# RWKV time mixing on one core: decay and rate products on 128 rows, and the chain's keys and deltas stacked over 128 rows

## The chip, the cores and the metric

The kernel runs on one core of one Trainium2 chip. The metric is the device time in microseconds of one execution; several executions are made and the median is taken. The profile is of one execution, taken by the hardware profiler.
## The reference, cut to what matters

The model has two layers over 256 context and 512 latent tokens of width 1024: layer 0 is grouped-query attention, layer 1 bidirectional RWKV-7 time mixing, each followed by an MLP. The change lies in the RWKV part of layer 1:

```python
w_log = -softplus(-(w0 + tanh(xw @ w1) @ w2)) - 0.5     # two directions n, rank 64
a = sigmoid(a0 + (xa @ a1) @ a2)                        # two directions, rank 64
k_dir = k * (1 + (a - 1) * k_a)
decay = exp(-exp(w_log))
def step(S, inp):                                       # per direction and head (16 heads of 64)
    w_t, k_t, v_t, a_t, b_t = inp[:5]                   # a_t = -kk, b_t = kk * a
    sa = einsum('dbhij,dbhj->dbhi', S, a_t)
    S = S * w_t + sa[:, None] * b_t + v_t[:, None] * k_t
    return S, einsum('dbhij,dbhj->dbhi', S, inp[5])     # times r
```

The decay product is `tanh(xw @ w1) @ w2` with `w0` added, the rate product is `(xa @ a1) @ a2`. The state takes two outer products, one of the keys with the values and one of `b` with the deltas `sa`.

## The kernel before

The RWKV core works through 16 units q: 8 groups g of 128 channels (two heads) times two directions d. The scan is done in 12 chunks of 64 tokens (`C = 64`), two chunks `cp` to a tile `m` of 128 tokens. Each unit goes through three stages, and `slots` runs them shifted against each other: slot s holds `pre(s)`, `inverse(s - 1)` and `chain(s - 2)`. The order inside a slot is written out by hand in two strings `SLOT` of the letters p, i and c; at each letter every engine emits its next piece of that stage. So every engine's queue has this fixed order, and each waits by semaphores for the others. Slots 0 to 15 have a pre stage, the chain runs alone at the end.

`pre` (lines 882 to 1096): PE makes the decay product into PSUM. `w0` goes in as a product of a row of ones with `W0G` on one row of the array (L890), and `W2G` times the tanh tile `LW` on 64 rows adds to it (L894): the two directions lie in the upper and lower 64 partitions of `LW`, `LA`, `W2G` and `A2G`, and each q takes its half. ACT takes the tanh (L984), PE makes the rate product on the same 64 rows (L901), ACT its tanh (L988), PE the cumulative product over the tokens of a chunk (L908, 128 rows), ACT two exponentials. HEAD1 sums squares (L917), VG is transposed (L925) and copied by ACT into `VT` (L1008). DVE makes BT = kk * a * WI and KD = k_dir * WI; PE transposes both into `BKT` (L934, L942) and multiplies them with `AR` into the 64x64 matrices of `MT` (L958), which DVE masks (L1093). L971 multiplies `MT` with V into `LV`.

`inverse` (L1119 to L1163): 19 rounds of 64x64 products (L1124, L1129, L1144) with copies by DVE (`UM`) and ACT. Neighbours stand in different quarters of the array.

`chain` (L1208 to L1255) walks through the 12 chunks. Each step has three pieces. First, `AR` times the state `SS` (L1224), and DVE adds `LV` to give `RH`. Second, the inverse times `RH` gives the deltas (L1236), DVE copies them to `SA` (L1318), and in the shadow of that copy PE multiplies keys and V into the state's PSUM (L1241). Third, PE waits for `SA`, adds its product with `BKT` (L1248), and for the last 8 chunks adds two products to the output, one with V (L1253) and one with `SA` (L1256). DVE makes the new `SS`. V and SA of one chunk stand on the same 64 partitions, so all of these products have 64 rows and 64 columns.

SP loads per group KG, W2G, A2G and W0G (counted by `ga_loaded`, L1461) and then VG, RG and G2G (L1466). The first load waits for the end of the low-rank products (`w_used`). POOL sets pads of `WP` to 1 at the start (L1507, L1508).

## Time and profile before

| | us |
|---|---|
| median of 3 runs | 2772.3 (2768.23 to 2775.69) |
| profiled execution | 2781.47, its span 2779.5 |
| TensorE busy | 2500.7 (90% of the span) |
| DVE, ACT, POOL busy | 1107.7, 952.6, 573.2 |
| mean granted clock of TensorE | 0.922 |

The RWKV core takes the stretch from about 1373 to 2340 us of the span. Times in the views are from the span's start. Ends of products are modelled, so neighbouring records overlap. In the timeline a row stands for one or more records of one line; in the chain of waits a row gives the piece of a group that lies on the chain.

### The profile page before, as it was taken

Reading aid. Unit: us, or ns where it says so; the run is one execution under the profiler, and the core shown is the slowest. Engines: PE = TensorE matmul, PEld = TensorE weight load, DVE = VectorE, ACT = ScalarE, POOL = GpSimd, SP = SyncE. Lnnn points to the kernel's source line nnn. Section 1 sums busy time; section 2 is a strip of 40 time slices with the busy share of each in tenths; the row PEclk is TensorE's granted clock in tenths of the full one; section 3 lists DMA queues with packets and bytes.
Section 4 is the critical chain, followed back from the end, with each engine's and each line's share of the span. In section 5 each row is a group of like instructions: output and inputs, shape, how many; then the busy total and the mean of one; then the engine's idle time right before and its main releaser. Section 6 shows DMA issues by size and latency. Waiting matters only on the chain.

```text
span 2779.5 us, 67680 instructions
## 1 busy us (share of the span) xinstructions
PE 2500.7 (90%) x28879; PEld 2062.0 (74%) x28879; DVE 1107.7 (40%) x2324; ACT 952.6 (34%) x1605; POOL 573.2 (21%) x361
## 2 busy tenths in 40 slices
PE   5989998899999998699678999998999986899998
PEld 4767777788888887587457777777777774788886
DVE  2235655231212122522735565555655553311112
ACT  3655555231212122222333334333332332323323
POOL 0320000222232322222111111111111101344442
PEclk9999999999999999799869899988988895999999
DMA  7225453211111211124100000000000001232331
GB/s 224 57 66 168 152 171 89 61 61 61 60 60 60 71 55 56 53 93 120 59 20 3 21 11 13 20 4 21 11 13 20 3 3 54 69 106 91 96 99 60
DMA packets 172290, 176.11 MB, mean 63 GB/s; under 512 B 26240, under 2 KB 159760, under 8 KB 172048
## 3 DMA queue, kind: packets, MB, share of 16 engines
q1 hardware_dynamic: 172048, 172.49, 19.8%
q8 instruction: 200, 3.28, 0.5%
q14 instruction: 42, 0.34, 0.0%
HBM read 160.93 MB, written 11.53 MB: 62 GB/s over the span
## 4 chain that ended last, share of the span: by engine, by line
PE 83%; DVE 9%; issue 4%; ACT 2%; DMA 1%; SPq 0%; POOL 0%; ACTq 0%; DVEq 0%; PEldq 0%
PE PS L379 43%; PE PS L1144 5%; PE PS L399 3%; PE PS L607 2%; PE PS L1129 2%; PE PS L958 2%; PE PS L634 2%; PE PS L901 2%; PE PS L908 2%; PE PS L1124 1%; PE PS L1248 1%; PE PS L1236 1%; PE PS L1224 1%; PE PS L586 1%; PE PS L894 1%
## 5 line engine op out<-in xcount | busy, mean ns | idle before, releaser
L359 POOL TENSOR_TENSOR WL<-RAW,WH 128x1024 fp32r<-128x1024 f32 x184 | 439.7, 2413 | 1340.6 <-ACT WH L353 1340.6
L379 PE MATMUL PS<-AH,WH 128*128 128x512 f32 (+1 forms) x1320 | 475.1, 360 | 84.0 <-DVE AL L824 38.4
L379 PE MATMUL PS<-AH,WL 128*128 128x512 f32 (+1 forms) x1320 | 473.8, 359 | 0.0
L379 PE MATMUL PS<-AL,WH 128*128 128x512 f32 (+1 forms) x1320 | 469.8, 356 | 0.0
L379 PEld LDWEIGHTS PS<-AH,WH 128*128 128x128 f32 x1320 | 253.9, 192 | 133.1 <-issue 55.2
L379 PEld LDWEIGHTS PS<-AL,WH 128*128 128x128 f32 x1320 | 252.7, 191 | 37.3
L379 PEld LDWEIGHTS PS<-AH,WL 128*128 128x128 f32 x1320 | 253.6, 192 | 33.9
L353 ACT ACTIVATE WH<-RAW 128x1024 fp32r<-128x1024 f32 x184 | 183.8, 1047 | 267.1 <-PE PS L379 265.5
L379 PE MATMUL PS<-BH,WL 128*128 128x512 f32 (+1 forms) x768 | 273.4, 356 | 0.0
L379 PE MATMUL PS<-BH,WH 128*128 128x512 f32 (+1 forms) x768 | 272.6, 355 | 0.0
L379 PE MATMUL PS<-BL,WH 128*128 128x512 f32 (+1 forms) x768 | 271.5, 353 | 0.0
L549 DVE SCALAR_TENSOR_TENSOR X<-PS,MOD,X 128x256 f32 (+3 forms) x120 | 72.0, 656 | 447.2 <-PE PS L379 447.2
L1144 PE MATMUL PS<-XI,MT 64*64 64x64 f32 x3840 | 189.9, 233 | 7.4 <-issue 6.1
L1129 PE MATMUL PS<-XIT,UM 64*64 64x64 f32 x3840 | 180.5, 226 | 16.0 <-issue 15.8
L525 DVE TENSOR_TENSOR HSQ<-HRL 128x768 f32<-128x768 f32 (+1 forms) x64 | 51.2, 841 | 332.6 <-ACT HRL L513 332.6
L1144 PEld LDWEIGHTS PS<-XI,MT 64*64 64x64 f32 x3840 | 160.1, 144 | 17.8 <-issue 17.3
L1129 PEld LDWEIGHTS PS<-XIT,UM 64*64 64x64 f32 x3840 | 146.1, 136 | 23.9 <-issue 23.7
L379 PEld LDWEIGHTS PS<-BH,WH 128*128 128x128 f32 x768 | 144.9, 189 | 21.9
L379 PEld LDWEIGHTS PS<-BL,WH 128*128 128x128 f32 x768 | 144.4, 188 | 21.4
L1174 ACT ACTIVATE XI<-PS 128x256 f32<-128x256 f32 x192 | 73.5, 383 | 251.6 <-PE PS L1129 251.5
L379 PEld LDWEIGHTS PS<-BH,WL 128*128 128x128 f32 x768 | 144.7, 188 | 20.2
L1111 POOL TENSOR_TENSOR MT<-MT,CT 128x256 f32<-128x256 f32 x48 | 34.9, 727 | 575.3 <-DVE MT L1093 575.3
(239 smaller groups left out, 4601.5 us busy)
## 6 DMA issues: line engine op xcount, KB each, us to landing
ADW<-l_ada_w SPq DMA_DIRECT2D x40, 1024.0 KB, 5.3
RAW<-l_mlp_up SPq DMA_DIRECT2D x64, 512.0 KB, 4.3
RAW<-l_mlp_down SPq DMA_DIRECT2D x64, 512.0 KB, 4.0
RAW<-l_w_rkv SPq DMA_DIRECT2D x24, 512.0 KB, 4.7
rwkv_scratch<-STG SPq DMA_DIRECT2D x24, 384.0 KB, 2.7
ADA<-l_ada_w SPq DMA_DIRECT2D x4, 2048.0 KB, 15.8
RAW<-l_w_in SPq DMA_DIRECT2D x16, 256.0 KB, 5.4
RAW<-l_w_out SPq DMA_DIRECT2D x16, 256.0 KB, 5.1
```

Source lines behind the costliest of these rows:

```text
L353: e.activation(WH[:, s, rows], RAW[:, s, rows], ACT.Copy).then_inc(w_high[h], 1)
L359: e.tensor_tensor(WL[:, s, rows], RAW[:, s, rows], WH[:, s, rows], ALU.subtract).then_inc(w_split[h], 1)
L379: mm = e.matmul(dst, w[:, s, k, n * P:(n + 1) * P], r[:, k, lo:hi], start=(k == 0 and i == 0), stop=(k == KT - 1 and i == 2), skip_group_c ...
L399: mm = e.matmul(dst, w[:, s, k, n * P:(n + 1) * P], r[:, k, lo:hi], start=(k == 0 and i == 0), stop=(k == KT - 1 and i == 2), skip_group_c ...
L549: ins = e.scalar_tensor_tensor(out=x, in0=tile_ps(4 * s + 2 * n)[:, a0:a1], scalar=gate, in1=x, op0=ALU.mult, op1=ALU.add)
L607: mm = e.matmul(pair(2 * j)[:, a0:a1], QS[:, g % 2, j, r * P:(r + 1) * P], kk[:, j, a0:a1], start=(i == 0), stop=(i == 1), skip_group_chec ...
L634: mm = e.matmul(bank(7)[64 * j:64 * j + 64, 0:P], VF[:, 2 * p + j, l, :], PTS[:, m % 2, b, :], start=(l == 0), stop=(l == nb - 1), skip_gr ...
L901: mm = e.matmul(tile_ps(3)[:, a0:a1], A2G[r, :], LA[r, a0:a1], start=True, stop=True, skip_group_check=True)
L908: mm = e.matmul(pair(3)[:, m * P:(m + 1) * P], SG[:, m, :], table(f"cum{d}"), start=True, stop=True, skip_group_check=True)
L1129: return e.matmul(bank(2)[o if v < 15 else HALVES[cp], i * C:(i + 1) * C], UM[o, v % 2, i, :], XIT[o, 4 * (v % 3) + i, :], start=True, sto ...
L1144: mm = e.matmul(bank(0)[o, i * C:(i + 1) * C], MT[b][t, u, 0, 0, :], XI[t, u, :] if n >= 3 else IDN[t, t], start=True, stop=True, skip_gro ...
L1174: e.activation(XI[:, four, :].rearrange("p u t -> p (u t)"), bank(1)[:, 0:256], ACT.Copy).then_inc(xi_ready, 1)
```

## The change

The two directions get tiles of their own, filled up with zeros: `LW[d]` is [128, T], with the tanh on its own 64 partitions, a row of ones on the first partition of the other half and zeros elsewhere; `W2X[:, d]` has `w2` on the same 64 rows and `w0` on the row of the ones. `A2X[:, d]` has `a2` on 64 rows and zeros on the others. The product of the ones is gone, and decay and rate products use all 128 rows. POOL makes the zeros and ones, and SP and ACT wait for it (`PADS = 12`); SP's loads per group go from 4 to 7 for `ga_loaded`. The LW tanh becomes two on 64 partitions each.

In the chain, `VSA` has a slot for each chunk with V on one half of the partitions and the deltas on the other. BT and KD are laid out as `KB` so that in `BKT` each chunk has keys on V's half and BT on the deltas' half, and `MT` has its output matrices stacked in the same way. State and output products of a chunk become one each with 128 rows in place of two with 64. To put the deltas there, `RH`, `LV`, the inverse's operands and the results move to the other half. The V copy becomes two ACT instructions of 64 partitions, `UM` moves into unused places of `AR`, masks grow by 128 columns for each direction, and `AA = KK * AA` is made in place.

```diff
 def pe_pre(e, q):
-    e.wait_ge(ga_loaded, 64 * (g + 1) + 16)
+    e.wait_ge(ga_loaded, 112 * (g + 1) + 16)
-    for m0, m1 in ((0, 4), (4, NTT)):
-        e.matmul(pair(3)[:, m0 * P:m1 * P].rearrange("p (m c) -> p m c", c=P), ONES[0:1, :],
-                 W0G[0:1, d, :].unsqueeze(1).to_broadcast([1, m1 - m0, P]), start=True, stop=False,
-                 skip_group_check=True)
-        for m in range(m0, m1):
-            mm = e.matmul(pair(3)[:, m * P:(m + 1) * P], LW[r, m * P:(m + 1) * P], W2G[r, :], start=False,
-                          stop=True, skip_group_check=True)
+    for m in range(NTT):
+        mm = e.matmul(pair(3)[:, m * P:(m + 1) * P], LW[d][:, m * P:(m + 1) * P], W2X[:, d, :], start=True,
+                      stop=True, skip_group_check=True)
...
-        mm = e.matmul(tile_ps(3)[:, a0:a1], A2G[r, :], LA[r, a0:a1], start=True, stop=True, skip_group_check=True)
+        mm = e.matmul(tile_ps(3)[:, a0:a1], A2X[:, d, :], LA[:, a0:a1], start=True, stop=True, skip_group_check=True)
...
-                for i, src in enumerate((BT, KD)):
-                    for cp, t in enumerate(HALVES):
+                for i in range(2):
+                    for cp in range(2):
                         c = 2 * m + cp
                         for h, k in enumerate(HEADS):
-                            mm = e.matmul(bank(3 + h)[t, i * P:i * P + wide * C], src[k, c * C:(c + 1) * C],
-                                          AR[b][k, c, 0:wide, :].rearrange("p a t -> p (a t)"), start=True, stop=True,
-                                          skip_group_check=True)
+                            out = bank(3 + h)[HALVES[1 - cp] if i == 0 else HALVES[cp], :].rearrange("p (z t) -> p z t", t=C)
+                            mm = e.matmul(out[:, i:i + 1, :] if wide == 1 else out[:, i:3 + cp:2 + cp - i, :],
+                                          KB[k, m, 1 + cp if i == 0 else 3 * cp, :], AR[b][k, c, 0:wide, :], start=True,
+                                          stop=True, skip_group_check=True)
 def act_pre(e, q):
-                e.activation(VT[gp][:, :, :].rearrange("p m c -> p (m c)"), pair(3)[:, 0:T], ACT.Copy).then_inc(vt_ready, 1)
+                for cp, t in enumerate(HALVES):
+                    ins = e.activation(VSA[gp][t, cp::2, :], pair(3)[t, 0:T].rearrange("p (m c) -> p m c", c=P), ACT.Copy)
+                ins.then_inc(vt_ready, 1)
 def pe_chain(e, q):
-                if j < NCH - 1:
-                    for k in HEADS:
-                        e.matmul(bank(6)[k, P:P + HD], BKT[b][t, m, 1, k], VT[gp][t, m, k], start=True, stop=False,
-                                 skip_group_check=True)
                 yield
                 e.wait_ge(sa_ready, 12 * q + j + 1)
                 e.nop(nofuse=True)
                 if j < NCH - 1:
                     for k in HEADS:
-                        mm = e.matmul(bank(6)[k, P:P + HD], BKT[b][t, m, 0, k], SA[t, k], start=False, stop=True,
+                        mm = e.matmul(bank(6)[k, P:P + HD], BKT[b][:, m, cp, k], VSA[gp][:, c, k], start=True, stop=True,
                                       skip_group_check=True)
                     mm.then_inc(st_done, 1)
                 if j >= NCH - NX:
                     for h, k in enumerate(HEADS):
-                        e.matmul(bank(7)[k, out_cols], VT[gp][t, m, k], MT[b][t, 2 * m + h, 1, 1, :], start=False,
-                                 stop=False, skip_group_check=True)
-                    for h, k in enumerate(HEADS):
-                        mm = e.matmul(bank(7)[k, out_cols], SA[t, k], MT[b][t, 2 * m + h, 0, 1, :], start=False,
+                        mm = e.matmul(bank(7)[k, out_cols], VSA[gp][:, c, k], mt(b, 2 * m + h, 2 + cp), start=False,
                                       stop=(d == 1), skip_group_check=True)
 def _(sp):
+            sp.wait_ge(pads_ready, PADS)
...
-                                     (W2G[:, :], a["l1_w2"].rearrange("d r c -> (d r) c")[:, cols]),
-                                     (A2G[:, :], a["l1_a2"].rearrange("d r c -> (d r) c")[:, cols]),
-                                     (W0G[:, :, :], a["l1_w0"][:, cols].unsqueeze(0))):
+                                     (W2X[0:64, 0, :], a["l1_w2"][0, :, cols]),
+                                     (W2X[64:128, 1, :], a["l1_w2"][1, :, cols]),
+                                     (W2X[64:65, 0, :], a["l1_w0"][0:1, cols]),
+                                     (W2X[0:1, 1, :], a["l1_w0"][1:2, cols]),
+                                     (A2X[0:64, 0, :], a["l1_a2"][0, :, cols]),
+                                     (A2X[64:128, 1, :], a["l1_a2"][1, :, cols])):
 def _(act):
-            act.activation(LW[:, :], tile_ps(0), ACT.Tanh).then_inc(evac_act, 1)
+            act.wait_ge(pads_ready, 4)
+            act.activation(LW[0][0:64, :], tile_ps(0)[0:64, :], ACT.Tanh)
+            act.activation(LW[1][64:128, :], tile_ps(0)[64:128, :], ACT.Tanh).then_inc(evac_act, 1)
```

## Rows read from the trace of the kernel before

**Rows 1.** The page: TensorE's clock in 40 slices, and the chain by engine.
```profile
PEclk9999999999999999799869899988988895999999
...
PE 83%; DVE 9%; issue 4%; ACT 2%; DMA 1%; SPq 0%; POOL 0%; ACTq 0%; DVEq 0%; PEldq 0%
```

**Rows 2.** The chain of waits, rate product L901 (start us, us, what, records).
```profile
1385.96 2.94 PE PS L901 x4
...
1475.65 2.85 PE PS L901 x4
...
2206.50 2.85 PE PS L901 x4
```

**Rows 3.** Windows: A:B length, busy PE PEld DVE ACT POOL, clock, DMA share, GB/s.
```profile
1476.00:2206.00 730.00, 667.18 (x15523) 553.10 (x15524) 422.82 (x1074) 259.56 (x520) 97.12 (x123) 0.88 0.05 13
1746.00:1750.50 4.50, 4.50 (x49) 3.10 (x47) 0.91 (x3) 0.60 (x2) 3.60 (x5) 1.00 0.01 4
1750.50:1753.50 3.00, 3.00 (x49) 2.74 (x49) 1.75 (x6) 0.81 (x1) 0.00 (x0) 0.52 0.00 0
...
1758.00:1760.90 2.90, 2.90 (x14) 2.63 (x13) 0.63 (x2) 0.00 (x0) 0.00 (x0) 0.51 0.02 6
1760.90:1765.00 4.10, 4.08 (x137) 3.73 (x136) 2.80 (x9) 2.75 (x6) 0.00 (x0) 1.00 0.00 0
1430.00:1440.00 10.00, 9.39 (x80) 7.06 (x79) 2.21 (x5) 2.17 (x3) 0.00 (x0) 0.50 0.01 2
2296.00:2332.00 36.00, 25.23 (x270) 19.93 (x268) 11.84 (x44) 0.00 (x0) 0.00 (x0) 0.51 0.01 1
```

**Rows 4.** Timeline of PE through one decay product (start us, us, line, form, records).
```profile
1746.99 1.12 PE L890 MATMUL PS<-W0G,ONES 1*128 1x512 f32 x2
1748.04 1.16 PE L894 MATMUL PS<-W2G,LW 64*128 64x128 f32 x8
...
1750.39 0.27 PE L1224 MATMUL PS<-SS,AR 64*64 64x64 f32 x2
```

**Rows 5.** Groups by line: the decay product's (busy us, mean ns).
```profile
L894 PE MATMUL PS<-W2G,LW 64*128 64x128 f32 x192 | 37.3, 339 | 0.0
...
L890 PE MATMUL PS<-W0G,ONES 1*128 1x512 f32 (+1 forms) x64 | 34.2, 619 | 6.3 <-DMA W0G<-l_w 5.7 <-ACT LV L1031 0.4
```

**Rows 6.** Timeline of PE around L917, a product on 128 rows.
```profile
1708.89 0.33 PE L1248 MATMUL PS<-SA,BKT 64*64 64x64 f32 x4
1709.15 1.56 PE L917 MATMUL PS<-TB,CK 128*128 128x256 f32 x4
1710.64 0.27 PE L1124 MATMUL PS<-UM,XIT 64*64 64x64 f32 x1
...
1710.80 0.22 PE L1124 MATMUL PS<-UM,XIT 64*64 64x64 f32 x1
...
1710.86 0.22 PE L1124 MATMUL PS<-UM,XIT 64*64 64x64 f32 x1
```

**Rows 7.** Timeline of PE in one third piece of the chain.
```profile
1766.28 0.33 PE L1248 MATMUL PS<-SA,BKT 64*64 64x64 f32 x4
1766.42 0.25 PE L1253 MATMUL PS<-MT,VT 64*64 64x64 f32 x2
...
1766.53 0.22 PE L1256 MATMUL PS<-MT,SA 64*64 64x64 f32 x1
```

**Rows 8.** Waits from 1476 to 2206 us (us in total, times, longest).
```profile
PE PS L1248 <- DVE SA L1318: 4.0, 11, 0.4
```

**Rows 9.** Groups by line: the V copy on ACT.
```profile
L1008 ACT ACTIVATE VT<-PS 128x768 f32<-128x768 f32 x8 | 6.5, 809 | 10.4 <-PE PS L925 10.4
```

**Rows 10.** Timeline of all engines at the core's start.
```profile
1373.07 0.34 SPq L1451 DMA_DIRECT2D CT<-table  x1
...
1375.50 0.73 SPq L1461 DMA_DIRECT2D W0G<-l_w  x1
...
1378.73 2.04 PE L890 MATMUL PS<-W0G,ONES 1*128 1x512 f32 x2 [5.75 <-DMA W0G<-l_w]
```

More of the change, by code:

```diff
@@ L222, in build @@
         VG, RG = two("VG", [P, T]), two("RG", [P, TX])
-        W2G, A2G, G2G = core("W2G", [P, P]), core("A2G", [P, P]), two("G2G", [P, P])
-        W0G = core("W0G", [1, 2, P])
+        W2X, A2X, G2G = core("W2X", [P, 2, P]), core("A2X", [P, 2, P]), two("G2G", [P, P])
         KK = core("KK", [P, T])
         WI = core("WI", [P, T])
-        bt_at = core_at[0]
-        SG = core("SG", [P, NTT, P])
-        BT = place("BT", bt_at, [P, T])
-        kd_at = core_at[0]
+        SG = place("SG", core_at[0], [P, NTT, P])
+        KB = core("KB", [P, NTT, 4, C])
         AA = core("AA", [P, T])
-        KD = place("KD", kd_at, [P, T])
         TB = core("TB", [P, T])
-        UM = core("UM", [P, 2, 4, C])
         XI = core("XI", [P, 12, C])
@@ L237, in build @@
         RKS = two("RKS", [P, TX])
-        VT = two("VT", [P, NTT, P])
+        VSA = two("VSA", [P, NCH, P])
         AR = three("AR", [P, NCH, 2, C])
@@ L242, in build @@
         BKT = three("BKT", [P, NTT, 2, P])
-        MT = three("MT", [P, 12, 2, 2, C])
+        MT = three("MT", [P, 40 * C])
+        UM = [AR[b][:, 0:4, 1, :] for b in (1, 2)]
         LV = three("LV", [P, NTT, P])
@@ L859, in chunks, with mt_at, mt, lta @@
             return ap.rearrange("p (c t) -> p c t", t=C)
-        def lta(b, u0, u1):
-            return MT[b][:, u0:u1, 0, 0, :]
+        def mt_at(u):
+            m, h = divmod(u, 2)
+            return 256 * m + 128 * h if m < TC // P else 512 * (m - 1) + 256 * h
+        def mt(b, u, part):
+            return MT[b][:, mt_at(u) + part * C:mt_at(u) + part * C + C]
+        def lta(b, u0):
+            end = mt_at(u0 + 4) if u0 < 8 else 40 * C
+            return MT[b][:, mt_at(u0):end].rearrange("p (u z) -> p u z", u=4)[:, :, 0:C]
         HEADS = (slice(0, 64), slice(64, 128))
@@ L1184, in dve_inverse @@
                     i = n % 3
[L1185 removed]
+                    dst = UM[n % 2] if n >= 3 else XI[:, 4 * i:4 * i + 4, :]
                     e.wait_ge(u_done, 18 * q + n + 1)
@@ L1504, in _ @@
                     pool_split(pool, 2 * i + s, s)
+            for d in range(2):
+                pool.memset(LW[d][:, :], 0.0).then_inc(pads_ready, 1)
+            pool.wait_ge(pads_ready, 2)
+            pool.wait_ge(w_split[1], U_OUT1 + 2)
+            pool.memset(LW[0][64:65, :], 1.0).then_inc(pads_ready, 1)
+            pool.memset(LW[1][0:1, :], 1.0).then_inc(pads_ready, 1)
             pool.wait_ge(w_used, U_LORA + 4)
+            pool.wait_ge(pads_ready, 4)
+            for w in (W2X, A2X):
+                pool.memset(w[:, :, :], 0.0).then_inc(pads_ready, 1)
             for b in range(3):
```

84 lines of the change are left out of this document (44 added, 40 removed).

## Prediction

> **What bounds the kernel now.** I began with the page. TensorE carries 83% of the chain that ended last, and its clock row is full except in the RWKV part [rows 1]. The change touches nothing else, so I went to that part. In the chain of waits, the rate product (L901) stands once in each slot, so it measures the slot: 13 slots lie between the starts of its first and last row shown, (2206.50 - 1475.65) / 13 = 56.2 us each [rows 2]. The windows view then says what a slot is made of [rows 3]. From 1476 to 2206 TensorE is busy 667 of 730 us, so it is the bound; its clock averages 0.88. The clock has two levels, 1.2 and 2.4 GHz, so the share at 1.2 GHz is 2 x 0.12, which is 175 us or 13.5 us a slot. While the clock is low TensorE is busy all the time (3.00 of 3.00, 2.90 of 2.90), so what falls into it is paid at double price. At the high clock it idles 63 of 555 us, 11%.
>
> Where is the clock low? In one slot [rows 3], it is 1.00 while the decay product runs, 0.52 right behind it, 0.51 through the cumulative product L908, and 1.00 after that; the rate product L901 lies in between. The stretch from 1430, which holds L901 and L908 of the second slot, has 0.50. L901's rows are as long at the end of the stretch as at its start, 2.85 [rows 2]. So the clock falls at or just after the decay product, and comes back at L908, the first product on all 128 rows. The decay product is K=1 and K=64 work: L890 uses one row of the array, L894 and L901 use 64 [rows 4]. The inverse and the chain use 64x64 tiles, several side by side, and hold 1.00 for long stretches (1760.9 to 1765). My reading, a theory so far: before the clock falls the engine works on few rows with no neighbour beside it, and before it rises it works on all rows.
>
> **The change, part by part, for one steady slot.**
>
> *Decay product.* It goes from 16 issued rows (L890 four, L894 twelve; each fp32 product is two records) to the twelve of L894, now on 128 rows. Before: in the timeline it runs from 1746.99 to the next product at 1750.39, 3.4 us [rows 4]. In all slots L890 and L894 are busy 34.2 + 37.3 = 71.5 us [rows 5]; less some 7.5 for the first slot, over 15 that is 4.3, and 4.1 without the overlap of the two. After: eight L894 rows take 1.16 us from first start to last end [rows 4], so a start each 0.11; four more give 1.6, or 1.5 to the next start. Rows used don't lengthen a row: L917 on 128 rows streams its 768 columns in 1.5 us [rows 6]. -2.6 us (ends -1.9 and -2.8).
>
> *Rate product.* Same columns, 128 rows in place of 64. Before 2.85 us, in the low stretch [rows 2, 3]. After, if the clock holds, it is L917's 1.5 [rows 6]. -1.35.
>
> *Cumulative product (L908), not touched.* 2.86 us low, [rows 3] has its window; 1.5 at the high clock by the same 0.11 a start. -1.35.
>
> *The rest of the low time.* 13.5 us less 2.85, 2.86 and about 1.2 of the decay product leaves 6.6; half is 3.3. At the high clock the waits on ACT and DVE come out from under it, 11% and about half a microsecond between rate and cumulative product, where the tanh on ACT is late next. -2.5 (ends -1.5 and -3.3).
>
> *Falls that remain.* Slots also begin with a wait for instructions, and the chain alone can thin the work; I add back 2.8 us of low time a slot. +1.4 (0 to +3).
>
> *V products of the chain (L1241, L1253) removed.* 11 + 8 = 19 pairs for each q. In one step L1248, L1253 and L1256 start 0.14 and 0.11 apart [rows 7], so a pair is worth 0.12: -2.3. As they use half the rows and the inverse can run beside them, the lower end is half of that; the upper is with low clock in it (-1.1 to -2.9).
>
> *Change of array shape, added.* This is what the diff does not say. Third pieces of the chain become 128x64 while all around them is 64x64. At a change of shape the trace shows the array emptied: L1248 ends at 1709.22 by its row and the 128-row L917 starts at 1709.15, and L917 ends at 1710.71 and the 64x64 rows start at 1710.64, 0.07 before it each time. Inside one shape, rows 0.22 long start 0.06 after the group before, an overlap of 0.16, and the first row behind a change is 0.27 long, not 0.22, while it waits for weights [rows 6]. So one change costs 0.09 + 0.05 = 0.14 us. Twelve steps with a way in and a way out are 24 changes, 3.4 us. Little of it is covered: TensorE waited for SA before L1248 only 11 times, 4.0 us in 13 slots [rows 8]; those waits and neighbours that change shape anyway take off a tenth. No row shows a 128x64 product in this part, so the bounds are half the price (covers I do not see) and 0.25 each, if the inverse's four tiles side by side fill slowly again: +3.1 (+1.2 to +6).
> The Trainium skill, TensorEngine Tiling (Array Packing), Key Properties, says that switching tiling mode drains TensorE while switching tile does not. The rows above agree with it and give it its price here; without the drain this part would be a gain of 2.3 us a slot instead of a loss of 0.8, some 47 us over the kernel. By that rule this half of the change works against itself.
>
> *Products that stay.* A pair on all rows can't have the inverse beside it: 19 x 0.03 = +0.5 (0 to +1.1).
>
> *Small things.* The V copy on ACT becomes two on half the partitions; time goes by columns, so +0.81 us every second slot [rows 9]. ACT is busy 260 of 730 us [rows 3], so half of it is covered: +0.2. The pairwise products of L958 meet the same tile twice in a row: +0.2. On DVE, sizes stay the same; the write of UM in runs of 64 and KB likewise: 0, covered by DVE's 42% idle. (ends 0 and +0.8 together)
>
> Sum: -2.6 - 1.35 - 1.35 - 2.5 + 1.4 - 2.3 + 3.1 + 0.5 + 0.4 = -4.7 us a slot; over the 15 slots with a decay product after the first, -71.
>
> *First slot and start.* The clock is low throughout and the work waits step by step, so only the decay product counts: it starts at 1378.73 [rows 10] and the rate product follows at 1385.96 [rows 2], 7.2 us later; twelve rows at the low clock need about 3, as L908 does: -4.2. Against that, KG and the rest now wait for POOL's zeroing and there are seven loads in place of four. The last of four was issued at 1375.50, 2.4 us behind CT, the three more at 0.5 us each: +1.8, as TensorE waited for just that load. The wait stands on SP, and VG, RG and G2G queue behind it, which are wanted only behind the cumulative product. The LW tanh in two halves adds 0.8 on ACT, hidden by the same wait of 5.75 us. Net -2.4. The added loads of later groups are issued half a slot ahead: 0.
>
> *Tail.* From 2296 the chain runs alone at 0.51 [rows 3]. There the array is empty between steps anyway, so neither the changes nor the V products count (they run under the copy of SA): 0 to +2, taken as +0.5.
>
> Sum: -73 us. The profiled execution took 2781.5 us (span 2779.5 and 2.0 around it), 9.2 over the median 2772.3. 2781.5 - 73 = 2708.5, and against the median **2699**.
>
> **Rivals.**
> 1. *The clock keeps falling.* The low clock may come from the waits at the slot's head, not from the rows in use. For: from 1430 the clock is 0.50 with TensorE busy 9.4 of 10 us, so busy alone doesn't lift it. Against: it is 1.00 during the decay product and falls behind it, with no idle time between (4.50 of 4.50) [rows 3]. Then the decay product gives -1.9 and the chain +1.7 with the small things: -0.2 a slot, -5 in all, **2767**.
> 2. *Changes of shape are cheap.* If the changes hide behind waits (+1.2 in place of +3.1) and no falls remain: -4.7 - 1.9 - 1.4 = -8.0 a slot, -122 in all, **2650**. For: DVE and TensorE alternate in the chain. Against: the 11 waits [rows 8].
> 3. *The slower side: emptying the array.* Its place is the third chain piece, 24 times a slot; at 0.25 us each it costs 6.0, and thinned work leaves the clock low at the slot's head. 6.0 + 0.9 - 2.3 - 1.9 = +2.7 a slot, +40: **2812**. With the clock regained it decides only from (4.7 + 3.1) / 24 = 0.33 us a change, over twice what the trace shows; with the clock still low, from (1.9 + 2.3 - 0.9) / 24 = 0.14, which is just the price read. The Trainium skill's rule named above (TensorEngine Tiling (Array Packing), Key Properties) is what this rival rests on; it gives no price. Against: 0.14 was read at two places, and the clock was 1.00 in dense 64x64 work.
> The change does what it says in every rival but the first, where the 128 rows leave the clock as it is.
>
> **How the numbers follow.** Forecast 0.68, rival 1 0.12, rival 2 0.12, rival 3 0.08. A measurement here tells about 0.3%, 8 us, from no change. The forecast and rival 2 are faster, rival 1 straddles (0.03 faster, 0.05 same, 0.04 slower), rival 3 is slower: faster 0.83, same 0.05, slower 0.12. The unknown terms (rest of low time 0.9, falls 1.5, V 0.9, changes 2.4, others 0.7) add as squares to 3.2 us a slot, 49 us: 2650 to 2748. That holds nearly all of the forecast and half of rival 2, about 0.75 to 0.8; I keep it, with the lower end at 2648, so that rival 2's own time lies inside.
>
> **What would show it.** Right: the clock at 1.00 through L901 and L908 in most slots, average near 0.97 between slots; the decay product 1.5 us; L901's place 1.5; slots near 51.5 us. In the third chain pieces every first 128x64 row starts 0.07 before the modelled end of the row before. Wrong: the clock at 0.50 behind a decay product on 128 rows (rival 1); slots below 49 (rival 2); starts after a change more than 0.2 us late, or new low windows in the middle of a slot (rival 3).

## The result and the profile after

| | before | after |
|---|---|---|
| median, us | 2770.3 (2765.31 to 2775.69, 4 runs) | 2663.2 (2662.41 to 2667.09, 4 runs) |
| ratio of the two, 95% interval | | 0.9611, 0.9593 to 0.9629 |
| profiled execution's span, us | 2779.5 | 2661.4 |
| mean granted clock | 0.922 | 0.957 |
| one steady slot, us | 56.2 | 48.5 |

The kernel became 107 us faster; 73 were forecast. The spans differ by more, 118 us, since the profiled execution of before lay 11 us over its median and that of after at it. The page of after, with the clock in 40 slices and the chain by engine [rows 1]:

```profile
span 2661.4 us, 65202 instructions
...
PEclk9999999989999999799988999999999977899999
...
PE 81%; DVE 10%; issue 4%; ACT 3%; DMA 1%; SPq 1%; POOL 0%; ACTq 0%; DVEq 0%; PEldq 0%
```

TensorE still carries the chain. The low digits that stood in the RWKV part are gone but for its start (8, 8) and its end (7, 7, 8); the 7 in the 17th slice lies ahead of that part, in both kernels. The chain of waits has the rate product, now L903, once a slot [rows 2]; the decay product is L896, the cumulative one L910 (start us, us, what, records):

```profile
1379.78 2.91 PE PS L896 x12
1383.58 2.94 PE PS L903 x4
...
1461.23 1.49 PE PS L903 x4
...
2087.62 1.53 PE PS L896 x12
...
2091.59 1.49 PE PS L903 x4
...
2094.23 1.53 PE PS L910 x12
```

(2091.59 - 1461.23) / 13 = 48.5 us a slot, 7.7 less. The windows show where it came from [rows 3]; the first is the 13 slots, the next three hold one slot's decay, rate and cumulative product (the first of them with small products of inverse and chain behind it), the last is the chain alone at the end:

```profile
1461.20:2091.50 630.30, 568.74 (x14484) 476.58 (x14482) 419.86 (x1075) 265.21 (x527) 101.60 (x125) 0.99 0.05 15
...
1797.50:1801.50 4.00, 3.65 (x60) 3.16 (x57) 2.33 (x8) 0.81 (x1) 2.88 (x4) 1.00 0.02 4
1801.50:1803.20 1.70, 1.70 (x15) 0.89 (x14) 0.53 (x2) 0.11 (x1) 0.00 (x0) 1.00 0.00 0
1804.20:1805.80 1.60, 1.60 (x16) 1.48 (x16) 0.90 (x3) 0.03 (x1) 0.00 (x0) 1.00 0.00 0
...
2179.00:2217.00 38.00, 24.48 (x193) 17.26 (x194) 12.77 (x45) 0.00 (x0) 0.00 (x0) 0.51 0.00 1
```

The clock rose from 0.88 to 0.99 and TensorE's busy time fell by 98 us in 13 slots, while DVE (422.8 and 419.9) and ACT (259.6 and 265.2) stayed. Summed over the stretches in which the trace's clock is at the low level, that level took 13.7 us of a slot before and 0.8 after. After has three falls in 13 slots, all in the middle of a slot, some 15 us behind the rate product. Before had 17: one at the head of each slot and four of 3.4 us in the middle.

In time, from the span's start to the end of the core's last product with `G2G` (119.9 us shorter in all): 2.4 up to the first rate product, 5.1 and 6.9 in the next two slots, 13 times 7.73 in the steady ones, 5.0 behind the last rate product.

### The profile page after: what moved, and what is told of

The parts are those of the page before. It is cut to its first block, busy times and chain, and to the rows that moved or that the text cites. A ratio compares the mean times of both kernels' runs of the same rounds, so it can differ in the third digit from the quotient of the medians.

```text
span 2661.4 us, 65202 instructions
## 1 busy us (share of the span) xinstructions
PE 2376.8 (89%) x27599; PEld 1966.4 (74%) x27599; DVE 1103.5 (41%) x2324; ACT 959.5 (36%) x1614; POOL 580.2 (22%) x367
## 4 chain that ended last, share of the span: by engine, by line
PE 81%; DVE 10%; issue 4%; ACT 3%; DMA 1%; SPq 1%; POOL 0%; ACTq 0%; DVEq 0%; PEldq 0%
PE PS L375 45%; PE PS L1154 4%; PE PS L395 3%; PE PS L603 2%; PE PS L1139 2%; PE PS L1254 2%; PE PS L630 2%; PE PS L962 2%; PE PS L1134 2%; PE PS L582 1%; PE PS L1246 1%; PE PS L612 1%; PE PS L1234 1%; DVE SMS L737 1%; PE PS L896 1%
## 5 line engine op out<-in xcount | busy, mean ns | idle before, releaser
L375 PEld LDWEIGHTS PS<-AL,WH 128*128 128x128 f32 x1320 | 251.9, 191 | 37.2
L1139 PE MATMUL PS<-XIT,AR 64*64 64x64 f32 x3840 | 173.3, 225 | 12.0 <-issue 11.9
L1154 PE MATMUL PS<-XI,MT 64*64 64x64 f32 x3840 | 170.6, 224 | 4.5 <-issue 3.2
L1154 PEld LDWEIGHTS PS<-XI,MT 64*64 64x64 f32 x3840 | 142.1, 136 | 19.3 <-issue 14.5
L1139 PEld LDWEIGHTS PS<-XIT,AR 64*64 64x64 f32 x3840 | 139.6, 135 | 21.9 <-issue 20.4
```

The lines of the kernel that those rows point to most:

```text
L375: mm = e.matmul(dst, w[:, s, k, n * P:(n + 1) * P], r[:, k, lo:hi], start=(k == 0 and i == 0), stop=(k == KT - 1 and i == 2), skip_group_c ...
L1139: return e.matmul(bank(2)[o if v < 15 else HALVES[cp], i * C:(i + 1) * C], UM[v % 2][o, i, :], XIT[o, 4 * (v % 3) + i, :], start=True, sto ...
L1154: mm = e.matmul(bank(0)[o, i * C:(i + 1) * C], mt(b, u, 0)[t], XI[t, u, :] if n >= 3 else IDN[t, t], start=True, stop=True, skip_group_che ...
```

## The experiments

All numbers of a slot are means over the 13 slots between the third and the sixteenth rate product of the one execution that was profiled, in us; "low clock" and "TensorE busy" are us of that slot. Ratios are against runs of the kernel before on the same chip.

| kernel | median us | ratio, 95% interval | slot | low clock in it | TensorE busy |
|---|---|---|---|---|---|
| before | 2770.3 | | 56.2 | 13.7 | 51.4 |
| after | 2663.2 | 0.9593 to 0.9629 | 48.5 | 0.8 | 43.8 |
| pre_only | 2677.1 | 0.9613 to 0.9680 | 49.5 | 0.5 | 44.2 |
| chain_only | 2766.2 | 0.9943 to 0.9979 | 54.9 | 12.1 | 50.2 |
| decay64 | 2665.3 | 0.9567 to 0.9636 | 48.7 | 0.3 | 43.6 |
| rate64 | 2664.4 | 0.9569 to 0.9635 | 48.5 | 0.3 | 43.8 |
| no_ones | 2684.8 | 0.9631 to 0.9687 | 49.7 | 0.8 | 44.3 |
| ones_added_1row | 2707.2 | 0.9717 to 0.9784 | 50.7 | 1.8 | 45.8 |
| ones_added_128row | 2689.1 | 0.9638 to 0.9696 | 50.1 | 1.1 | 45.2 |
| ones_decay64_rate128 | 2744.0 | 0.9848 to 0.9894 | 53.7 | 8.5 | 49.0 |
| first_on_64rows | 2694.9 | 0.9686 to 0.9742 | 49.8 | 0.0 | 44.9 |
| shape_added | 2715.2 | 0.9758 to 0.9793 | 51.7 | 1.6 | 47.3 |
| same_shape_added | 2688.5 | 0.9660 to 0.9692 | 50.2 | 0.5 | 45.1 |
| tail_fill | 2656.4 | 0.9543 to 0.9583 | 48.8 | 0.5 | 43.7 |

### The two halves apart

**pre_only** is the kernel before with the 128-row decay and rate products alone (and what they need: zero-filled tiles, seven loads a group, `UM` in `AR`); the chain is as it was.

```diff
-            for m0, m1 in ((0, 4), (4, NTT)):
-                e.matmul(pair(3)[...], ONES[0:1, :], W0G[0:1, d, :]..., start=True, stop=False)
-                for m in range(m0, m1):
-                    mm = e.matmul(pair(3)[...], LW[r, m * P:(m + 1) * P], W2G[r, :], start=False, stop=True)
+            for m in range(NTT):
+                mm = e.matmul(pair(3)[...], LW[d][:, m * P:(m + 1) * P], W2X[:, d, :], start=True, stop=True)
...
-                mm = e.matmul(tile_ps(3)[:, a0:a1], A2G[r, :], LA[r, a0:a1], ...)
+                mm = e.matmul(tile_ps(3)[:, a0:a1], A2X[:, d, :], LA[:, a0:a1], ...)
```

> The kernel before with the 128-row decay and rate products alone (zero-filled LW, W2X and A2X, the seven loads, UM in AR); the chain stays as it was, with V and delta products on 64 rows. Theory A (the prediction's prices: the clock gives the whole gain, the change of array shape eats the removed V products): per slot -2.6 -1.35 -1.35 -3.0 +0.4 = -7.9, about -120 us, 2650 us, at or below the changed kernel's 2663. Theory B (changes of shape are mostly covered, the chain's merge is worth about 1.5 us a slot): per slot -6.2, about 2677 us, above the changed kernel. Both expect the clock near 0.99 between the second and the last slot.

**chain_only** is the kernel after with both products put back: the ones on one row, then 64 rows, and the rate product on 64 rows.

```diff
-            for m in range(NTT):
-                mm = e.matmul(pair(3)[...], LW[d][:, ...], W2X[:, d, :], start=True, stop=True)
+            for m0, m1 in ((0, 4), (4, NTT)):
+                e.matmul(pair(3)[...], LW[d][one:one + 1, 0:P], W2X[one:one + 1, d, :]..., start=True, stop=False)
+                for m in range(m0, m1):
+                    mm = e.matmul(pair(3)[...], LW[d][r, ...], W2X[r, d, :], start=False, stop=True)
...
-                mm = e.matmul(tile_ps(3)[...], A2X[:, d, :], LA[:, a0:a1], ...)
+                mm = e.matmul(tile_ps(3)[...], A2X[r, d, :], LA[r, a0:a1], ...)
```

> The changed kernel with decay and rate products put back on 64 rows, the product of the ones included (its row of ones and w0 are taken from LW and W2X); state and output products stay stacked on 128 rows. Theory A: the clock falls at each decay product as before, the chain costs +1.3 to +1.7 us a slot: 2770 + 20 to 25 = 2790 to 2795 us. Theory B: the merge gains 1.0 to 1.5 us a slot: 2748 to 2755 us. If the clock stays near 1.00 at the slots' heads although the decay product is on few rows again, the reading of the clock is wrong: below 2700 us.

Measured: 2677.1 us for the first half, 99.6 less than before (2776.6 in that set), and 2766.2 for the second, 10.4 less. The two gains add up to 110, about what the whole change gave (107), so to some us they don't lean on each other. In the chain of waits of chain_only the low clock is back; decay (L897 and L901), rate (L908) and cumulative product (L915) of one slot:

```profile
1800.36 1.05 PE PS L897 x2
1801.41 1.09 PE PS L901 x8
...
1807.02 2.85 PE PS L908 x4
...
1811.41 2.69 PE PS L915 x12
```

What follows: about 90% of the gain is the decay and rate products and the clock. The chain's half is a small gain, where a loss was forecast.

### What makes the clock fall

Each of the next seven kernels changes the head of the slot alone. decay64, no_ones and first_on_64rows leave `w0` out.

**decay64**: after, with the decay product on 64 rows and no product of the ones.

```diff
-                mm = e.matmul(pair(3)[...], LW[d][:, ...], W2X[:, d, :], start=True, stop=True)
+                mm = e.matmul(pair(3)[...], LW[d][r, ...], W2X[r, d, :], start=True, stop=True)
```

> The changed kernel with the decay product alone on 64 rows, without the product of the ones: w0 is left out of the result, everything else is as in the changed kernel, and the number of issued rows is the same twelve. Rows theory (the clock falls because few rows of the array are in use): the clock falls at the decay product again and comes back at the rate product, which has 128 rows, so for about 7 us of each slot: +2.5 to 3.5 us a slot, 2700 to 2715 us. Ones theory (only the product on one row pulls the clock down, or only the longer time of sixteen rows): the clock holds, 2660 to 2670 us.

**rate64**: after, with the rate product on 64 rows.

```diff
-                mm = e.matmul(tile_ps(3)[...], A2X[:, d, :], LA[:, a0:a1], ...)
+                mm = e.matmul(tile_ps(3)[...], A2X[r, d, :], LA[r, a0:a1], ...)
```

> The changed kernel with the rate product alone on 64 rows; same columns, same number of issued rows, same result. If the fall starts at the decay product alone, the clock holds through the rate product, which then takes the same 1.5 us as on 128 rows: 2660 to 2672 us. If 64 rows for 1.3 us are enough by themselves, the clock falls in each slot until the cumulative product: +2 to +3 us a slot, 2695 to 2710 us.

Measured: 2665.3 and 2664.4 us, neither to be told from after, with 0.3 us of low clock a slot in both. So the reading that 64 rows are too few fell for either product alone: one or the other on 64 rows changes nothing. What decay64 lacks against chain_only is the product of the ones, hence the next kernel.

**no_ones**: the kernel before, less the four issued rows of L890.

```diff
-            for m0, m1 in ((0, 4), (4, NTT)):
-                e.matmul(pair(3)[...], ONES[0:1, :], W0G[0:1, d, :]..., start=True, stop=False)
-                for m in range(m0, m1):
-                    mm = e.matmul(pair(3)[...], LW[r, ...], W2G[r, :], start=False, stop=True)
+            for m in range(NTT):
+                mm = e.matmul(pair(3)[...], LW[r, ...], W2G[r, :], start=True, stop=True)
```

> The kernel before with one thing taken out: the product of the ones (L890), so w0 is left out of the result. Decay product on 64 rows, rate product on 64 rows, chain as before, no zero-filled tiles. Ones theory (the one-row product is what precedes the fall; 64 rows are enough to hold the clock): nearly the whole gain of pre_only, 6.0 to 7.0 us a slot, 2665 to 2685 us, clock 0.99 in the steady slots. Filling theory (the gain of pre_only needs the array filled over decay and rate product together): 64 rows in both let the clock fall again, gain 1.9 us a slot at most for the shorter product, 2740 us or more.

Measured: 2684.8 us, 91 less than before (2776.0 in that set), with the decay product on 64 rows (timeline) and the clock at 1.00 through it and behind it (windows):

```profile
1811.93 1.60 PE L890 MATMUL PS<-W2G,LW 64*128 64x128 f32 x12
```

```profile
1811.90:1813.50 1.60, 1.60 (x19) 1.45 (x15) 0.53 (x2) 0.00 (x0) 1.45 (x3) 1.00 0.00 0
1813.50:1820.00 6.50, 6.38 (x99) 4.98 (x100) 4.05 (x12) 1.74 (x3) 1.32 (x2) 1.00 0.02 4
```

Here both products are on 64 rows, and taking away one product of one row gives nearly all that pre_only gives (2677.1; the intervals overlap). The four that follow ask whether it is the one row, or the length of thin work.

**ones_added_1row** and **ones_added_128row**: after, with a dead product of the size of the old one ahead of the 128-row decay product, on one row or on all.

```diff
+            for m0, m1 in ((0, 4), (4, NTT)):
+                e.matmul(pair(3)[...], LW[d][one:one + 1, 0:P], W2X[one:one + 1, d, :]..., start=True, stop=True)
             for m in range(NTT):
                 mm = e.matmul(pair(3)[...], LW[d][:, ...], W2X[:, d, :], start=True, stop=True)
```

> The changed kernel plus a dead product of the ones on one row, 768 columns like L890, ahead of the decay product, which then overwrites its result; nothing is left out. Ones theory: the clock falls at the slots' heads again although decay and rate product have 128 rows; it comes back sooner, at the rate product: 1.4 us for the product itself and 2 to 4 us for the clock, 2710 to 2745 us. If the clock holds, the fall in the kernel before needed the decay product on 64 rows as well: 2684 us.

> The same dead product with the same 768 columns, but on 128 rows. It takes the same time on TensorE, so it separates rows from time: both theories expect the clock to hold and the product's own 1.4 us a slot, 22 us: 2680 to 2688 us. The difference to the run with one row is the clock alone. Were time the cause, both would be equally slow.

Measured: 2707.2 and 2689.1 us. On 128 rows the dead product costs 1.65 us a slot: 1.3 by its rows, the rest idle time and 0.3 us more of low clock. On one row it costs 0.55 more, and the low clock is 0.8 us longer, which at double price is 0.4 of that. The clock falls at the head of two of the 13 slots, where with 128 rows it falls at none and in before at all; the other falls of both kernels are of the mid-slot sort that after has too. So the one-row product can bring the clock down by itself, but seldom does. The profiled execution of ones_added_1row was its fastest, with a mean clock of 0.954; the other three had 0.948 to 0.951, so its typical low time is longer than the 1.8 of the table, by an estimate from these clocks about 1 us a slot in the middle ones and 2 in the slowest (2717.5 us).

**first_on_64rows**: decay64 with a dead product of that size ahead, on 64 rows.

```diff
-            for m in range(NTT):
-                mm = e.matmul(pair(3)[...], LW[d][:, ...], W2X[:, d, :], start=True, stop=True)
+            for m0, m1 in ((0, 4), (4, NTT)):
+                e.matmul(pair(3)[...], LW[d][r, 0:P], W2X[r, d, :]..., start=True, stop=True)
+                for m in range(m0, m1):
+                    mm = e.matmul(pair(3)[...], LW[d][r, ...], W2X[r, d, :], start=True, stop=True)
```

> The changed kernel, with the decay product in the form that let the clock fall (a broadcast product of 768 columns ahead, then the product on 64 rows), but with that first product on 64 rows in place of one. It leaves w0 out. The twin is ones_decay64_rate128: 2743.98 us, 8.5 us of low clock a slot, slots of 53.7 us. Theory 'one row': the fall needs a product that uses a single row of the array; with 64 rows in both, the clock stays near 1.00 (under 1.5 us of low clock a slot), slots near 50.2, as the added product on 128 rows gave 50.1, and the kernel takes about 2690 us, ratio about 0.968. Rival 'thin stretch': 64 rows are too few as well when the stretch without neighbours is 3.1 us long instead of 1.6; then the clock falls as in the twin, slots 53 to 54 us, about 2740 us, ratio about 0.987. A result between, 2700 to 2725, would say that both count: the clock falls in part of the slots.

**ones_decay64_rate128**: after, with the decay product of chain_only and the rate product on 128 rows.

```diff
-            for m in range(NTT):
-                mm = e.matmul(pair(3)[...], LW[d][:, ...], W2X[:, d, :], start=True, stop=True)
+            for m0, m1 in ((0, 4), (4, NTT)):
+                e.matmul(pair(3)[...], LW[d][one:one + 1, 0:P], W2X[one:one + 1, d, :]..., start=True, stop=False)
+                for m in range(m0, m1):
+                    mm = e.matmul(pair(3)[...], LW[d][r, ...], W2X[r, d, :], start=False, stop=True)
```

> The changed kernel with the decay product alone put back as it was (ones on one row, then 64 rows), rate product on 128 rows; nothing is left out. The runs so far: neither half of the old decay product makes the clock fall by itself, both together do (chain_only: 12.1 us low a slot). If the fall belongs to the decay product's stretch and the rate product's rows bring it back, low time goes from 12.1 to about 6 to 8 us a slot and the time to 2665 + 15 x (1.9 + 3) = 2720 to 2745 us. If the rate product on 64 rows took part in the fall itself, the clock holds here: 1.9 us a slot for the longer decay product, about 2692 us.

Measured: 2694.9 and 2744.0 us. These two are twins that differ in how many rows the first product has, 64 or one (and in what these rows hold, and in that the second product adds to it; neither was varied alone). Windows over the 13 slots, first_on_64rows first:

```profile
1469.85:2117.48 647.63, 583.67 (x14536) 483.76 (x14535) 419.14 (x1075) 265.70 (x527) 99.59 (x123) 1.00 0.05 15
```

```profile
1473.40:2171.20 697.80, 637.25 (x14536) 514.29 (x14534) 420.63 (x1075) 265.99 (x527) 99.51 (x123) 0.92 0.05 14
```

The clock is 1.00 with 64 rows and 64 rows, and 0.92 with one row and 64 rows, though both stream the same columns. So the amount of work on 64 rows or fewer doesn't decide it by itself: what lets the clock fall at the head of every slot is the product on a single row together with one on 64 rows. With the second on 128 rows (ones_added_1row) it holds in most slots; with the first gone, or on 64 rows, at the head of all of them. The profiled execution of first_on_64rows was its fastest, though (2688.0 us, mean clock 0.958; the other three 2694.5 to 2697.6, 0.952 or 0.953), so 0.0 us of low clock is its best case; by an estimate from these clocks the others have up to 2 us more a slot. That is far from the twin's 8.5, and the twins' medians are 49 us apart.

The fall doesn't always wait for the second product. Ahead of the fifth rate product of before (timeline and windows) the clock was at 1.00 until 0.6 us into the one-row product and at 0.50 from 0.7 us on, before the first 64-row product had started:

```profile
1579.32 1.50 PE L890 MATMUL PS<-W0G,ONES 1*128 1x512 f32 x2
1580.75 2.07 PE L894 MATMUL PS<-W2G,LW 64*128 64x128 f32 x8
```

```profile
1579.30:1579.90 0.60, 0.60 (x6) 0.29 (x2) 0.57 (x2) 0.22 (x1) 0.60 (x1) 1.00 0.00 0
1580.00:1585.00 5.00, 5.00 (x16) 3.19 (x14) 1.41 (x4) 0.84 (x1) 4.01 (x6) 0.50 0.43 147
```

Over the 13 slots of before the falls at the head begin 0.6 to 4.7 us behind the start of the decay product, nine of them inside it. The two earliest (0.6 and 0.7) stand in slots where TensorE idled 1.2 us shortly ahead of it, as it does in every second slot. Such a wait is not enough: first_on_64rows has it too (1.0 us) and keeps the clock. Whether it helps a one-row product to bring the clock down was not tried.

ones_decay64_rate128 shows a second thing against chain_only, from which it differs in the rate product alone (chain of waits):

```profile
1796.23 2.86 PE PS L908 x4
1800.56 1.53 PE PS L915 x12
```

In this slot the rate product is still paid at the low clock, 2.86, but the cumulative product behind it takes 1.53 where chain_only has 2.69. The low clock lasts 8.5 us a slot in place of 12.1, and the kernel takes 22 us less. So rows in use do count where the clock is to rise: 128 rows in the rate product bring it back one product sooner. Once it no longer falls they are worth nothing (rate64).

### What the chain's half costs and gives

**shape_added** puts a dead 128x128 product ahead of each state product, so one more change of shape (64x64, 128x128, 128x64). **same_shape_added**, its control, puts a dead pair of the state product's own shape there.

```diff
                 if j < NCH - 1:
+                    e.matmul(bank(6)[:, P:P + HD], IDN[:, :], HEAD1[:, 0:HD], start=True, stop=True)
```

```diff
                 if j < NCH - 1:
+                    for k in HEADS:
+                        e.matmul(bank(6)[k, P:P + HD], IDN[:, k], HEAD1[:, 0:HD], start=True, stop=True)
```

> The changed kernel with a dead 128x128 product of 64 columns ahead of each state product in the third pieces (11 for each q), into the PSUM region that the state product then overwrites; nothing is left out. It adds one change of shape to each of these pieces. Theory of full price (0.14 us a change, not covered): 1.5 us a slot more than the run same_shape_added beside it, 24 us. Theory of cover (PE's waits and its overlaps take most of it): under 0.6 us a slot, 10 us.

> The control: a dead pair of 128x64 products of 64 columns at the same place, the shape of the state products behind it, so no change of shape is added. A pair by itself should cost 0.12 us, 11 of them 1.3 us a slot, 21 us: 2684 us. If part of the chain's gain came from fewer instructions, the waits without a releaser (issue) grow with the added ones: from 20 us in 13 slots toward 25 or more.

Measured: 2715.2 and 2688.5 us. The difference, 26.7 us over 11 x 16 = 176 places, is 0.15 us each, close to the price that rows 6 gave (0.14). Not all of it is the emptied array: the four executions of shape_added had mean clocks of 0.952 to 0.954, those of the control 0.958 to 0.960. Half a per cent of the clock is 1% of the time at the low level, some 27 us, and so up to 13 us of the 26.7; without it a place costs 0.08. In the 13 slots the low level took 1.1 us more of a slot. Whether the added changes of shape bring the clock down there is open. And by the rows only 9.2 changes of shape a slot came on top (44.1 against 34.9), not 11. So 0.15 us is what one added change costs this kernel all told, good to a factor of about two as the price of emptying the array. The control's dead pair costs (2688.5 - 2663.2) / 176 = 0.14. At the place itself (timelines, first shape_added, then its control; L1255 and L1257 are the state product):

```profile
1592.34 0.43 PE L1253 MATMUL PS<-CK 128*128 128x64 f32 x2
1592.70 0.34 PE L1255 MATMUL PS<-VSA,BKT 128*64 128x64 f32 x4
```

```profile
1762.10 0.34 PE L1254 MATMUL PS<-CK 128*64 128x64 f32 x4
1762.23 0.32 PE L1257 MATMUL PS<-VSA,BKT 128*64 128x64 f32 x4
```

The state product starts 0.36 us behind the first and 0.13 behind the second. Not all of the 0.23 is the change of shape: the dead 128-column product also has more weights to load (198 ns and 140 ns by the groups of the two kernels), and some of it hides under waits.
The Trainium skill, TensorEngine Tiling (Array Packing), Key Properties, says that changing the tiling mode drains TensorE. These runs agree, and in this kernel one more change costs 0.15 us, the clock's part included.

pre_only and after differ in the chain's half alone. Their groups over the 13 slots (busy us, mean ns of one, idle before), first pre_only, then after:

```profile
L1237 PE MATMUL PS<-VT,BKT 64*64 64x64 f32 x576 | 65.0, 231 | 1.7 <-issue 1.7
...
L1244 PE MATMUL PS<-SA,BKT 64*64 64x64 f32 x576 | 51.2, 236 | 7.5 <-DVE SA L1314 3.6 <-issue 2.4
...
L1249 PE MATMUL PS<-MT,VT 64*64 64x64 f32 x416 | 37.4, 222 | 0.9 <-issue 0.9
L1252 PE MATMUL PS<-MT,SA 64*64 64x64 f32 x416 | 36.8, 220 | 1.1 <-issue 1.1
```

```profile
L1254 PE MATMUL PS<-VSA,BKT 128*64 128x64 f32 x576 | 49.0, 245 | 12.9 <-DVE VSA L1321 7.9 <-issue 3.0
...
L1259 PE MATMUL PS<-MT,VSA 128*64 128x64 f32 x416 | 32.5, 228 | 0.2 <-issue 0.2
```

Four products become two of nearly the same length. Busy times of neighbours overlap, so I took for each row of the timeline the time from its start to the next start, and summed it by tile, in us a slot:

| | pre_only | after |
|---|---|---|
| keys and V, into the state and the output | 1.86 + 0.96 | gone |
| SA (VSA) into the state and the output | 1.79 + 1.17 | 2.28 + 1.97 |
| other products of chain and inverse | | +1.25 |
| pairwise matrices (L958 before) | 2.81 | 2.60 |
| TensorE idle | 5.30 | 4.74 |
| changes of array shape, number | 14.9 | 35.0 |

By this table the V products were worth 2.82. The merged ones take 1.29 more than the SA pairs alone, and their neighbours 1.25: 2.54 for 20 more changes of shape, 0.13 each if the changes are all of it (products that can't run beside the inverse would show in the same sum). With the pairwise matrices and the idle time that makes -2.82 + 2.54 - 0.21 - 0.56 = -1.05; the slots differ by 0.98. TensorE waits longer for the deltas, now that the V products don't stand ahead: 7.9 us in 24 waits, where pre_only had 3.6 in 10. It sits idle less in gaps for which the profile shows no cause ("issue": 19.6 us in place of 37.2), and that more than makes up for it. Why those gaps shrink is open. Fewer instructions go with it (14484 records in place of 15476), and the control's added pairs brought the gaps up to 29.1 us, as its expectation had it; but shape_added, with added products too, has 14.4. The state's merged product and the output's were not undone one by one, so how the gain splits between them is open too.

### The chain alone at the end

**tail_fill** is after with dead 64x64 products behind each piece of the last chain, to keep TensorE's clock up where the chain runs alone.

```diff
+            def filler():
+                if q == NQ - 1:
+                    for z in HALVES:
+                        for i, k in enumerate(HEADS):
+                            e.matmul(bank(i)[z, 0:P], IDN[k, 0:HD], HEAD1[k, :], start=True, stop=True)
...
+                filler()
```

> A try at a faster version: the changed kernel with dead products (four 64x64 tiles of 128 columns, into PSUM that nobody reads) behind each piece of the last chain, q = 15, which runs alone at 0.51 of the clock for 38 us. If they keep the clock at 1.00, each of its 34 small product groups is shorter by 0.15 us and the products behind it too: -4 to -8 us, about 2657 us. If they stand in the way of the chain instead (the next group waits behind them): 0 to +5 us.

```profile
2180.00:2212.00 32.00, 25.85 (x473) 16.64 (x474) 13.43 (x47) 0.00 (x0) 0.00 (x0) 1.00 0.01 2
```

Measured: 2656.4 us (2652.65 to 2661.13), against 2663.2, and the clock 1.00 where after has 0.51. The core's last product with `G2G` ends at 2212.6 in place of 2217.7, though its sixteenth rate product came 3.5 us later than after's. The intervals of the two ratios lie just beside each other (up to 0.9583, from 0.9593), but those of rate64 and decay64, which are as fast as after, overlap with it. So this is a likely gain of some 7 us by the medians; only one set of runs shows it.

## Why the prediction was right, and where it was off

The forecast was 2699, the time 2663.2: faster, as forecast, inside the range, and 36 us off. The main mechanism was right (the clock comes back when the decay product changes), its cause was half right, and the chain's half had the wrong sign. By the parts as they were put:

**Decay product, -2.6.** Right. L896 takes 1.53 where 3.4 to 4.1 stood, and in the groups of after its time less the first slot's is (26.9 - 2.9) / 15 = 1.6 us a slot, so -2.5:

```profile
L896 PE MATMUL PS<-W2X,LW 128*128 128x128 f32 x192 | 26.9, 292 | 7.6 <-DMA A2X<-l_a 6.9 <-ACT LV L1038 0.7
```

**Rate and cumulative product, -1.35 each.** Right: 1.49 and 1.53 in place of 2.85 and 2.86.

**Rest of the low time -2.5, falls that remain +1.4.** Low clock of 13.7 us a slot became 0.8, where 2.8 was allowed for. The sum of this half came out close: the parts up to here are -6.4 a slot, and with -2.4 at the start -98; pre_only, which is just them, gave -99.6 (-89 to -107 by its interval). That closeness is in part luck. pre_only has 0.5 us of low clock left, so the falls that remain cost 0.3 and not 1.4; its slot is 6.8 shorter, so with -2.5, -1.35 and -1.35 the rest of the low time gave only 1.8 of its 2.5, and about 1.1 against a median execution of before (see the end of this section). The two misses nearly cancel. The reason was half right as well. "Few rows with no neighbour" is not what lets the clock fall: 64 rows hold it. For a fall in every slot it takes the product on one row with the 64-row product behind it, and folding `w0` into the decay product is enough: rate64, with the rate product left on 64 rows, takes as long as after. That all rows help it to rise was right.

**V products -2.3, changes of shape +3.1, products that stay +0.5, small things +0.4: +1.7.** This is the step that failed, in size and in sign: after less pre_only is -0.98 a slot, 2.7 us off, and over 15 slots 40 us, which covers the miss of 36. The price of a change came out close (0.14 read, 0.15 measured, though part of the 0.15 is clock). The number of changes was wrong: 24 changes were counted as if each way in and out were new, and 20 came on top, as four of the twelve third pieces have a 128-row neighbour on one side. So changes and products that stay cost 2.5, not 3.6 (1.1 of the miss). The V products were worth 2.8, not 2.3 (0.5). The small things gave 0.2 in place of costing 0.4 (0.6); the V copy on ACT took its 0.8 more every second slot, and TensorE's idle time did not rise for it:

```profile
L1014 ACT ACTIVATE VSA<-PS 64x768 f32<-64x768 f32 x16 | 12.9, 803 | 9.7 <-PE PS L927 9.7
```

And 0.6 came from idle time, which I had left as it was.

**The start, -2.4.** Right as a sum: the rate product came at 1383.58, 2.4 earlier. Two misses cancel in it: the decay product started 1.05 later than before, where 1.8 was forecast, and from there to the rate product it took 3.4 less, where 4.2 was. As the prediction had it, the product waited for the load that was named, the last of seven (timeline):

```profile
1379.78 2.90 PE L896 MATMUL PS<-W2X,LW 128*128 128x128 f32 x12 [6.90 <-DMA A2X<-l_a]
```

**The tail, +0.5.** Small, as forecast; behind the last rate product 5.0 us went, but that stretch holds a slot's remainder with a cumulative product and chain work beside the inverse. The chain alone has the same 0.51 as before.

**What would show it.** The clock, the decay product and the rate product came as written (1.00, 1.53, 1.49). The starts around a third piece are as written too; here it stands between 64x64 work and the rate product (timeline of after):

```profile
2090.64 0.68 PE L1154 MATMUL PS<-CK,MT 64*64 64x64 f32 x16 [0.33 <-DVE XI L1197]
2091.26 0.34 PE L1254 MATMUL PS<-VSA,BKT 128*64 128x64 f32 x4
2091.52 1.56 PE L903 MATMUL PS<-LA,A2X 128*128 128x256 f32 x4
```

L1154 ends at 2091.32 by its row and L1254 starts at 2091.26; L1254 ends at 2091.60 and L903 starts at 2091.52: 0.06 and 0.08 before it. The rows also show why the count was too high: L903 changes the shape at this place in either kernel, so this piece adds one place at which the shape changes, not two.

**The rivals.** The first (the clock keeps falling, 2767) is out: 1.00 through the head of the slot. The second (changes of shape are cheap, 2650) named slots below 49, and they came, 48.5. One of its two conditions held, that no falls remain; the other did not hold as put: the changes do not hide, there are fewer of them than counted, and other terms gave more. That its time was closer than the forecast (2650 against 2699) is thus in part luck. The third, the slower side, is out: a change is 0.15 us, under the 0.33 from which it decides with the clock up.

The prediction also read the page's clock row as full except in the RWKV part; it has a 7 in its 17th slice, ahead of that part and untouched by the change. Nothing rests on it.

The 118 us by the spans hold 11 us of the execution of before that happened to be profiled. Executions of before differ in their low clock: of thirteen in one set the shortest, 2764.2 us, had a mean clock of 0.929 and the longest, 2788.6, one of 0.921; the profiled one had 0.922. At 0.926, about a median execution's, 2 x 0.004 x 2780 = 22 us less are low, which is 11 us of time, or 0.7 a slot. So the slots saved about 7.0 against a median execution, not 7.7.

## What to carry to other kernels

Look for products with a tiny contraction (a bias brought in by a row of ones): they take as long as a full one (rows below), and here one of them, together with a half-filled product behind it, halved the clock for a quarter of every slot; put the row into the operand of the next product instead. Before a merged product is charged with changes of array shape, count the changes that come on top of those the neighbours make anyway, and price one from the trace (0.15 us here). When the forecast has two halves, run each alone: the sum here was 36 us off, and one half alone by two. And compare the clock of the profiled execution with that of the others before its low time is called typical.

## What the runs showed of the hardware

- TensorE's clock fell from 1.00 to 0.50 while it was busy without a gap. At the head of every slot it fell only with a product on one row followed by one on 64 rows: 13.7, 12.1 and 8.5 us of low clock a slot (before, chain_only, ones_decay64_rate128). With 128 rows in the second place it fell at two heads of 13 (1.8 us a slot), with 64 rows in both at none (0.0), and without the first product at none (0.3 to 0.8, from falls in the middle of slots, which nearly every kernel here shows now and then). These are single executions.
- With the rate product on 128 rows the low clock ended sooner than with the same product on 64 rows: 8.5 and 12.1 us a slot, 2744.0 and 2766.2 us.
- At the high clock a product on 64 rows takes as long as on 128, by form over the 13 slots of rate64 and of after:

```profile
L903 PE MATMUL PS<-LA,A2X 64*128 64x512 f32 x26 | 13.2, 589 | 0.0
```

```profile
L903 PE MATMUL PS<-LA,A2X 128*128 128x512 f32 x26 | 13.3, 592 | 0.0
```

- A product of 512 columns on one row takes as long as on 128, by form over all slots of ones_added_1row and of ones_added_128row:

```profile
L897 PE MATMUL PS<-W2X,LW 1*128 1x512 f32 x32 | 18.9, 671 | 7.9 <-DMA A2X<-l_a 7.0 <-ACT LV L1043 1.0
```

```profile
L897 PE MATMUL PS<-W2X,LW 128*128 128x512 f32 x32 | 18.9, 673 | 7.8 <-DMA A2X<-l_a 6.9 <-ACT LV L1043 0.8
```

- One more change of the array's shape costs 0.15 us in the kernel's time, of which up to half can be clock; a pair of small dead products costs 0.14.
